# Indirect transfers and turned rows in place of selection matmuls for six of eight experts

## The reference

```python
def moe_swiglu(h, router, w_in, w_out):        # h = rms_norm(x, ffn_norm[1])
    t = h.reshape(b * s, d)
    logits = (t @ router).astype(jnp.float32)
    top_vals, top_idx = lax.top_k(logits, TOP_K)
    gates = jax.nn.softmax(top_vals, axis=-1)
    combine = jnp.sum(jax.nn.one_hot(top_idx, N_EXPERTS) * gates[..., None], axis=1)
    for e in range(N_EXPERTS):
        y = y + combine[:, e:e + 1] * swiglu(t, w_in[e], w_out[e])
```

## Time and profile before

| | us |
|---|---|
| median of 3 runs | 1492.41 (1492.3 to 1493.67) |
| the profiled execution, its own time | 1492.52 |
| its span in the trace | 1490.4 |
| PE busy | 1463.7 (98%) |
| DVE busy | 1208.6 (81%) |
| ACT busy | 995.7 (67%) |
| POOL busy | 132.8 (9%) |

### The profile page before, as it was taken

How to read it: one execution, slowest core, us unless ns; L and a number is a source line. 1 busy time by engine, 2 the same in 40 slices (tenths; PEclk the granted TensorE clock), 3 DMA queues, 4 the chain that set the end, 5 groups by cost and what they waited for, 6 DMA issues and landing times.

```text
span 1490.4 us, 19624 instructions
## 1 busy us (share of the span) xinstructions
PE 1463.7 (98%) x7818; PEld 1237.3 (83%) x7818; DVE 1208.6 (81%) x1031; ACT 995.7 (67%) x850; POOL 132.8 (9%) x201
## 2 busy tenths in 40 slices
PE   8999999999999999999999999999999999999998
PEld 7967888889998778888888888888888888888776
DVE  7976766666386799888888888888888888888997
ACT  5667444465546677777777777777777777777774
POOL 8505200000253000000000000000000000000200
PEclk9999999999999999999999999999999999999999
DMA  9504555546510399999999999999999999999994
GB/s 344 171 6 164 197 197 181 185 143 197 193 34 31 116 349 372 352 387 379 348 377 382 351 374 388 365 362 386 374 349 389 377 349 380 381 347 377 411 377 164
DMA packets 206919, 432.50 MB, mean 290 GB/s; under 512 B 6914, under 2 KB 56251, under 8 KB 206827
## 3 DMA queue, kind: packets, MB, share of 16 engines
q1 hardware_dynamic: 204880, 424.78, 78.2%
q0 software_dynamic: 1904, 6.46, 1.1%
q10 hardware_dynamic: 42, 0.01, 0.0%
HBM read 426.51 MB, written 4.72 MB: 289 GB/s over the span
## 4 chain that ended last, share of the span: by engine, by line
PE 92%; DVE 4%; ACT 2%; issue 1%; DMA 0%; DVEq 0%; SPq 0%; ACTq 0%
PE bank L1466 25%; PE bank L1468 25%; PE bank L1467 25%; PE bank L1507 6%; PE bank L1509 3%; PE bank L1739 2%; PE bank L1868 2%; PE bank L1820 1%; DVE w_l L294 1%; PE bank L1720 1%; DMA raw<-in_ab_w_in 0%; PE bank L1721 0%; ACT w_h L289 0%; PE bank L1567 0%; PE bank L1473 0%
## 5 line engine op out<-in xcount | busy, mean ns | idle before, releaser
L294 DVE TENSOR_TENSOR w_l<-raw,w_h 128x2048 fp32r<-128x2048 f32 x402 | 920.8, 2292 | 182.1 <-ACT w_h L289 181.4
L289 ACT ACTIVATE w_h<-raw 128x2048 fp32r<-128x2048 f32 x402 | 770.9, 1918 | 353.3 <-PE bank L1468 287.4
L1466 PE MATMUL bank<-w_h,hs_h 128*128 128x512 f32 x896 | 355.3, 397 | 3.7 <-DVE w_l L294 2.8
L1468 PE MATMUL bank<-w_h,hs_l 128*128 128x512 f32 x896 | 349.7, 390 | 0.0
L1467 PE MATMUL bank<-w_l,hs_h 128*128 128x512 f32 x896 | 349.0, 390 | 0.0
L1466 PEld LDWEIGHTS bank<-w_h,hs_h 128*128 128x128 f32 x896 | 168.3, 188 | 38.1 <-issue 3.3
L1468 PEld LDWEIGHTS bank<-w_h,hs_l 128*128 128x128 f32 x896 | 168.2, 188 | 36.0
L1467 PEld LDWEIGHTS bank<-w_l,hs_h 128*128 128x128 f32 x896 | 168.5, 188 | 33.2
L1466 PE MATMUL bank<-w_h,ma_h 128*128 128x512 f32 x448 | 174.6, 390 | 1.7 <-DVE w_l L294 1.7
L1467 PE MATMUL bank<-w_l,ma_h 128*128 128x512 f32 x448 | 174.3, 389 | 0.0
L1468 PE MATMUL bank<-w_h,ma_l 128*128 128x512 f32 x448 | 174.3, 389 | 0.0
(11 more groups left out here) (298 smaller groups left out, 1661.1 us busy)
## 6 DMA issues: line engine op xcount, KB each, us to landing
raw<-in_moe_w_in SPq DMA_DIRECT2D x224, 1024.0 KB, 5.7
raw<-in_moe_w_out SPq DMA_DIRECT2D x112, 1024.0 KB, 5.4
raw<-in_ffn_w_in SPq DMA_DIRECT2D x22, 1024.0 KB, 5.0
raw<-in_hgrn_w_in SPq DMA_DIRECT2D x16, 1024.0 KB, 5.1
raw<-in_ffn_w_out SPq DMA_DIRECT2D x11, 1024.0 KB, 4.7
raw<-in_ab_w_in SPq DMA_DIRECT2D x10, 1024.0 KB, 11.3
raw<-in_ab_w_out SPq DMA_DIRECT2D x4, 1024.0 KB, 4.8
raw<-in_hgrn_w_out SPq DMA_DIRECT2D x4, 1024.0 KB, 4.9
```

Source lines behind the costliest of these rows:

```text
L289: act.activation(w_h[:, u0 % S, :], raw[:, u0 % R, :], ACT.Copy).then_inc(w_high, 1)
L294: eng.tensor_tensor(w_l[:, u0 % S, :], raw[:, u0 % R, :], w_h[:, u0 % S, :], ALU.subtract).then_inc(w_low, 1)
L1466: pe.matmul(o, a_high, b_high, start=start, stop=False, skip_group_check=True)
L1468: return pe.matmul(o, a_low, b_high, start=False, stop=stop, skip_group_check=True)
```

## The change

- Early on POOL, three direct transfers copy `x` over most of a new tensor `x_rows` in device memory (768 rows).
- After the norm, ACT writes the scaled, ungained tokens to `xn` (`token_norm`). DVE works out for each token the slots of its two experts (`slots`, 14 small operations in step 0 of the first expert; a token without a slot gets a spare row). POOL sends `xn` to `x_rows` by four indirect transfers, waits for them, and loads 128 rows for each of the experts 1 to 6 into `x_g`, the first two at once, the others behind the writes of `y_rows`.
- For experts 1 to 6 PE turns those rows (`turn_rows`, eight transposes) in place of the 48 matmuls. Experts 0 and 7 are gathered as before; the first gather goes to four banks.
- The gain is put on behind the turning or the gather: `gather_high` and `gather_low` are eight operations of 128 columns with a scale each, where they were two of 512. The three bf16 parts are of ungained tokens; the third is made by POOL.
- The router reads `x` itself, turned, with the gain multiplied into its weights ahead of time and the norm applied to its 16 sums. The fillers `keep_warm` of the norm are gone and the eight after the router are four.
- `gates`, `slots`, `overflow`, `combine` and `rows` stand in steps 0 to 3 of the first expert, and ACT's Exp in step 1.

Cut to its core, with the lines that say the same for other buffers left out:

```diff
             n_const["all"] = made[0]
+            for b in range(3):
+                pool.dma_start(x_rows[CAP + b * T:CAP + (b + 1) * T, :], A["x"][0]).then_inc(x_fill, 16)
...
+            for tt in range(TT):
+                pool.wait_ge(x_mid, tt + 1)
+                pool.tensor_tensor(x_b[:, 2, tt, :], x_g[:, tt, :], x_b[:, 1, tt, :], ALU.subtract).then_inc(x_low, 1)
+            pool.wait_ge(x_norm, TT)
+            pool.wait_ge(x_fill, 16 * 3)
+            for k in range(2):
+                pool.wait_ge(slot_ok, k + 1)
+                for tt in range(TT):
+                    pool.indirect_dma_start(out=x_rows, out_offset=bass.IndirectOffsetOnAxis(ap=slot_i[:, k, tt:tt + 1], axis=0),
+                                            in_=xn[:, tt, :], in_offset=None).then_inc(x_sent, 16)
+            pool.wait_ge(x_sent, 16 * 2 * TT)
+            def expert_rows(e):
+                pool.dma_start(x_g[:, e % 2, :], x_rows[e * CAP:(e + 1) * CAP, :]).then_inc(xe_in[e % 2], 16)
+            expert_rows(1)
+            expert_rows(2)
             for e in range(NR):
                 pool.wait_ge(y_cp, 2 * e + 2)
                 pool.dma_start(y_rows[e * P:(e + 1) * P, :], y_f[:]).then_inc(y_out, 16)
+                if e + 3 < NE - 1:
+                    pool.wait_ge(m_gat, 2 * (e + 1) + 4)
+                    expert_rows(e + 3)
+            pool.wait_ge(m_gat, 2 * (NR - 1) + 4)
...
+            def residual_router():
+                add_part(3, 0, 0)
+                add_part(3, 0, 1)
+                norm_eps(3, 0)
+                add_part(3, 1, 0)
+                norm_root(3, 0)
+                add_part(3, 1, 1)
+                turned(0)
+                turned(1)
+                norm_eps(3, 1)
+                turned(3)
+                norm_root(3, 1)
+                token_rest(0)
+                token_rest(1)
...
+                    step(dve.tensor_tensor(row_m[:, 1 + k, :, :], logit[:, 4 + k, :, :], row_m[:, 0, :, :], ALU.mult))
+                    step(dve.tensor_tensor(row_m[:, 3, :, :], row_m[:, 1 + k, :, :], row_f[:], ALU.mult))
+                    dve.tensor_reduce(row_v[:, k, :], row_m[:, 1 + k, :, :], AX.X, ALU.max).then_inc(r_d, 1)
+                    done[0] += 1
+                    step(dve.tensor_reduce(row_w[:, k, :], row_m[:, 3, :, :], AX.X, ALU.add))
+                    step(dve.scalar_tensor_tensor(out=row_v[:, 2 + k, :], in0=row_v[:, k, :], scalar=0.5, in1=spill_no[:, k, :],
+                                                  op0=ALU.is_lt, op1=ALU.mult))
+                    dve.tensor_tensor(slot_i[:, k, :], row_v[:, 2 + k, :], row_w[:, k, :], ALU.add).then_inc(slot_ok, 1)
...
+            def gather_low(n, b, banks=(5, 6)):
+                w = KC // len(banks)
+                for k in range(KC):
+                    if k % w == 0:
+                        dve.wait_ge(m_hh, n * KC + (k + w))
+                    dve.scalar_tensor_tensor(out=hs_l[:, b, k, :], in0=bank[:, banks[k // w], (k % w) * P:(k % w + 1) * P],
+                                             scalar=par[:, C_FFN + 8 + k:C_FFN + 9 + k], in1=hs_h[:, b, k, :],
+                                             op0=ALU.mult, op1=ALU.subtract).then_inc(m_hl, 1)
...
+                if j == 0 and turn[0] == 0 and first:
+                    gates()
+                    slots()
+                if j in (1, 2, 3) and turn[0] == 0 and first:
+                    (overflow, combine, rows)[j - 1]()
+                if j == 3 and turn[0] and not last:
+                    dve.wait_ge(m_pt, q)
+                    choose(e + 1, 1, 1 - hb)
+                if j == 3 and turn[0] == 0 and e == NE - 2:
+                    choose(NE - 1, 0, 1 - hb)
...
-            for tt in range(TT):
-                act.wait_ge(x_gain, TT + tt + 1)
-                act.activation(x_b[:, 1, tt, :], x_g[:, tt, :], ACT.Copy).then_inc(x_mid, 1)
+            table(ACT.Sqrt)
+            norm_square(3, 0, 0)
+            norm_square(3, 0, 1)
+            norm_rms(3, 0)
+            norm_square(3, 1, 0)
+            token_high(0)
+            norm_square(3, 1, 1)
+            norm_rms(3, 1)
+            act.wait_ge(x_t, 3)
+            act.activation(h_f[:, 1, 0:4, :], bank[:, 2, :].rearrange("p (c t) -> p c t", c=4), ACT.Copy).then_inc(r_act, 1)
+            token_high(1)
+            token_mid(0)
+            token_mid(1)
             split_high(act, U_MOE + 2)
...
                 moe_gate(s + 1, u0 + 1, rounds)
+                if j == 1 and turn[0] == 0 and first:
+                    act.wait_ge(r_d, n_const["exp"])
+                    act.activation(pick[:, 5, :], pick[:, 4, :], ACT.Exp).then_inc(r_e, 1)
+                    table(ACT.Silu)
...
-            norm_turn(3)
...
+            for tt in range(TT):
+                pe.wait_ge(x_add, 8 + 2 * tt + 2)
+                for b in range(2):
+                    for c in range(4):
+                        last = pe.transpose(bank[:, 2 * tt + b, c * P:(c + 1) * P], x[:, tt, (4 * b + c) * P:(4 * b + c + 1) * P], ident[:])
+                    last.then_inc(x_t, 1)
+            pe.wait_ge(r_gain, 1)
+            for tt in range(TT):
+                for c in range(KC):
+                    if c % 4 == 0:
+                        pe.wait_ge(*((r_act, 1) if (tt, c) == (1, 0) else (r_dve, 2 * tt + c // 4 + 1 - tt)))
+                    last = pe.matmul(bank[:, 5, tt * NE:(tt + 1) * NE], h_f[:, tt, c, :], router[:, c, :],
                                      start=c + tt == 0, stop=c == KC - 1, skip_group_check=True)
             last.then_inc(r_lg, 1)
-            keep_warm(8, 7)
...
+            def turn_rows(e):
+                pe.wait_ge(xe_in[e % 2], 16 * ((e + 1) // 2))
+                for i in range(2):
+                    for c in range(4):
+                        last = pe.transpose(bank[:, 5 + i, c * P:(c + 1) * P], x_g[:, e % 2, (4 * i + c) * P:(4 * i + c + 1) * P], ident[:])
+                    last.then_inc(m_gat, 1)
...
                     k = half * KH + c
+                    if fresh is not None:
+                        pe.wait_ge(m_hl, fresh * KC + (k + 1))
                     last = three(bank[:, b, :], hs_h[:, hb, k, :], hs_l[:, hb, k, :], wh[:, c, :], wl[:, c, :], k == 0, k == KC - 1)
...
-                                pe.wait_ge(m_hl, n * 2 + 2)
-                            gather(n + 1, 1 - hb)
+                                pe.wait_ge(m_hl, n * KC + KC)
+                            if turn[0] == 0 and e + 1 < NE - 1:
+                                turn_rows(e + 1)
+                            else:
+                                gather(n + 1, 1 - hb, q + 3 if turn[0] else 2)
```

More of the change, by code:

```diff
@@ L42 @@
 NR = NE - 1
+SLOTS = NE * CAP
 LAM_INIT = 0.8 - 0.6 * math.exp(-0.3 * 0)
@@ L211, in build @@
         y_in = [sem(f"y_in{tt}") for tt in range(TT)]
+        x_norm, slot_ok, x_sent, x_fill = (sem(k) for k in "x_norm slot_ok x_sent x_fill".split())
+        xe_in = [sem(f"xe_in{b}") for b in range(2)]
         stored = sem("stored")
@@ L354, in _ @@
                            allow_small_or_imprecise_dtypes=True))
+            step(pool.iota(spill_no[:], pattern=[[T, 2], [P, TT]], base=SLOTS, channel_multiplier=1,
+                           allow_small_or_imprecise_dtypes=True))
             n_const["early"] = made[0]
@@ L935, in choose, with slots @@
                                       ALU.is_equal).then_inc(m_sel, 1)
-            def rows():
+            def slots():
                 ranks = rank[:].rearrange("p (a e) -> p a e", a=TT)[:, :, 0:NE]
                 step(dve.tensor_scalar(row_m[:, 0, :, :], ranks, CAP + 0.5, None, ALU.is_lt))
-                dve.tensor_tensor(row_f[:], ranks, row_no[:].unsqueeze(1).to_broadcast([P, TT, NE]), ALU.add).then_inc(r_d, 1)
-                done[0] += 1
+                step(dve.tensor_tensor(row_f[:], ranks, row_no[:].unsqueeze(1).to_broadcast([P, TT, NE]), ALU.add))
@@ new lines, in slots, with rows @@
+                    done[0] += 1
[3 more added lines that the diff above has]
+                    dve.tensor_tensor(slot_i[:, k, :], row_v[:, 2 + k, :], row_w[:, k, :], ALU.add).then_inc(slot_ok, 1)
+            def rows():
+                for k in range(2):
@@ L1007, in moe_body @@
                     row_sums(j // 2)
[L1008 to L1012, removed]
-                    choose(e + 1, turn[0], 1 - hb)
+                if j == 0 and turn[0] == 0 and first:
[8 more added lines that the diff above has]
+                    choose(NE - 1, 0, 1 - hb)
                 split_low(dve, u0 + 5, rounds)
@@ L1045, in moe_round @@
                         split_low(dve, u + i)
[L1046 to L1054 removed]
+                    gather_low(n0, 0)
+                for i in (3, 4, 5):
                     split_low(dve, u + i)
@@ L1826, in rows @@
                 def rows(i, parts, first, final):
-                    for c in range(4):
-                        f = slice((4 * i + c) * P, (4 * i + c + 1) * P)
```

(4 more changed lines are left out.)

191 lines of the change are left out of this document (87 added, 104 removed).

## The result

The changed kernel takes 1507.57 us (median of 4 runs, 1506.87 to 1507.87) against 1492.79 for the kernel before in the same comparison: a ratio of 1.0093, 95% interval 1.0081 to 1.0106. The prediction was 1479.1, range 1475 to 1486, with 0.07 on slower. It was wrong in sign.

The account below looks back on a forecast made before the run. PE was taken as the bound, busy 958.06 of 962.5 us at full clock in the expert stretch. The terms summed as 1492.5 - 11.2 - 3.4 + 0.7 + 0.5 = 1479.1 us, range 1475 to 1486.

Parts of the forecast that it names:

- a cut in PE's own list is worth its full length there: Expert stretch, 962.5 us with PE busy 958.06: instructions removed from PE save their whole time if ACT, DVE and DMA keep up.
- Turns, -11.2: Experts 1 to 6: eight fp32 turns of 0.93 us replace a 2.80 us gather, saving 1.87 each, 11.2 us in all.
- The beat of 17.7: Sign of being right: steps that held a gather take 17.7 us between SP's issues instead of 19.6.
- Small copies, 0: Eight 128-wide copies each on ACT and DVE behind the turns stay covered: 0, or up to 1 us at seven experts.
- Head, -3.4: From the last residual add to the first gather: shorter DVE chain, less a slower clock; 3.4 us saved, bounds -4.8 to -0.5.
- the head gives nothing: Rival, chance 0.15: half clock through gather and first weights, or x_low late, cancels the head's saving: 1482.5 us, or 1485.
- Small work in the first expert, +0.7: Gates' small operations moved into the first expert's steps: stalls of 4.3 us less 3.6 lost today, 0.7 us added.
- waits for w_l near 2, 1.7 and 0.4: Sign of being right: PE's waits in us in expert 0, from small operations put ahead of weights.
- clock below 1 behind 512 us: Sign of being wrong: PE's clock not full after 512 us, about when the first expert's matmul was expected.
- Traffic, +0.5: Added scatters, row loads and early copies crowd the weight loads: 0.5 us added, bounds 0 to 4.
- Rows late: Rival, chance 0.05: scatters taking over 60 us hold PE at expert 1; beyond 13 us late the kernel is slower.
- DMA is the bound: Rival, chance 0.05: at 365 GB/s the turns save nothing and 5.2 MB more cost 14.3 us: 1503.4 us.

Follow-up runs that it names:

- experiment 1: The changed kernel with the unused spare tensor 32 bytes smaller per partition, so the stage tensors start again at multiples of 512 bytes: 1483.71 us.
- experiment 10: experiment 1 with x_low made by VectorE behind the first expert's selection instead of by GpSimd: 1479.51 us.
- experiment 9: Program of only 512-column matmuls, none of the reference's work, tiles at varied starts: 389 ns at 0 or 256 bytes apart, 392 at 192, 394 to 396 else.

## Why the prediction was wrong

The step that failed is the first: "a cut in PE's own list is worth its full length there", with the 16.80 us of an ordinary step and the 2.72 of a unit carried over from the trace of before. The list did get shorter, by what was forecast. But the sum took every matmul that stays at its old length, and looked for costs only in waits and in instructions added. The diff's `spill_no` line was costed as "POOL's one more iota and DVE's scaling of the router are done while those engines wait", that is by its time and not by its place. Its place lengthened some 4400 matmuls by 6 ns each, 24 us in all (experiment 1).

The account, in medians: 1479.1 predicted + 23.9 (experiment 1) + 4.2 (experiment 10) = 1507.2, measured 1507.57. It closes because experiment 10 lands on the forecast, and that is in part luck. Its profiled execution (1479.39 us) against the one before (1492.52) goes by four pieces: up to the first expert's matmul 515.47 - 512.46 = 3.0 us less (forecast 3.4); from there to the second expert's turns, which stand at

```profile
595.51 1.03 PE L1898 MATMUL bank<-ident,x_g 128*128 128x128 f32 x8
```

83.05 us where the gather came after 81.71, 1.3 more (forecast 0.7); from there to the end 882.2 for 893.2, 11.0 less (forecast 11.2 less 0.5 for traffic, 10.7); and 1.7 us outside the trace for 2.1. No piece is off by more than 0.7, but they cancel to 0.3. Point by point:

- *Turns, -11.2*: right. Eight turns cost 0.89 to 0.93 us over two steps, and the gather 2.80. The beat of 17.7 that was named as the sign was off in shape (17.95, then 16.58) and right in sum. One turn's record is 0.27 us long, but eight begin within 0.8 us: what counts is the distance of their starts.
- *Small copies, 0*: right. No wait for `hs_l` in experts 1 to 6.
- *Head, -3.4*: wrong as run, by one term. "x_low, which goes from DVE to POOL", was called hidden because PE comes to it late enough; what it does to DVE meanwhile was not asked. POOL's two operations took 2.2 each, as costed, but held up DVE's selection by 3.5 us (1.82 + 2.21 for 0.57), and by 3.1 in experiment 1. There the first expert starts at 515.51, as before the change (515.47): the outcome of the rival "the head gives nothing" (1482.5, measured 1483.71), by a cause that it didn't name. With that undone, the sums are read at 503.94 (forecast 504.8), the gather starts at 507.14 (508.0), and the first expert's matmul stands at 512.46 (512.1). Inside it, the clock was under-costed: the gather took 4.87 where 3.03 + 0.8 was taken. An earlier start paid for it.
- *Small work in the first expert, +0.7*: mis-sized: half of what came. The signs were waits for w_l near 2, 1.7 and 0.4. Experiment 10 has two in the first expert, 3.6 us of its 5.3, the longest 2.1, and the stretch above grew by 1.3. The changed kernel has 3.1 of its 4.3 there (its longer beat hides more). The fall of its clock behind the wait of 1.81 is one of the signs of being wrong that the prediction named ("clock below 1 behind 512 us"); it is worth 1.4 us, and the runs don't show why experiment 1 was spared.
- *Traffic, +0.5*: no cost seen. PE waits for nothing but DVE, and 374 GB/s in the expert stretch of experiment 1 stand against 365:

```profile
515.50:1468.00 952.50, 947.23 (x4335) 782.04 (x4336) 851.62 (x555) 718.66 (x526) 22.54 (x21) 1.00 1.00 374
```

- *Rows late*: no wait of PE for `x_g` in any trace.
- *The rival "DMA is the bound"*, 1503.4, lies nearest to the result and is the wrong reason. Anyone who had stopped at the number, at a DMA share of 0.99 and at an unchanged 365 GB/s in the changed kernel, would have taken it. But experiment 1 moved 374 GB/s with the same transfers, and the old kernel slowed down equally with none.

What stays open: why the 512-column matmuls of the dense layer (L1507, `w_h` stationary, `h_hl` moving), whose tiles begin a multiple of 512 bytes apart, take 398 ns in the kernel before, 394 with the weights moved, and 392 with only the stage tiles moved by 64 bytes, which neither of the two is. So the distance of the two tiles does not settle every case. Against the 399 with 32 bytes that is 352 x 7 ns = 2.5 us, the difference between those two runs; but with 128 bytes it is 396, and the time is no longer than with 64. Why 192 bytes cost only half was not tried. Nor was it tried whether POOL's work could stay on POOL if it began behind the selection.

## What to carry to other kernels

In a kernel at 98% PE, a new tensor can change every matmul whose tiles are allocated behind it: compare the mean ns of the unchanged matmuls before looking for waits, and add small tensors at the end of the allocation or in slots that keep the old starts. Moving work to an idle engine is free only if the operations that it runs beside are not on the path; name the other engine's instructions in that stretch and their operands. When a result agrees in size with one of the rivals, still undo that rival's cause alone.

## What the runs showed of the hardware

- fp32r matmuls of 512 columns, 128x128 stationary: 389 ns in the trace if the stationary and the moving tile start 0 or 256 bytes apart in SBUF (experiment 9, past a multiple of 512), 394 to 396 at most other distances tried (32, 64, 96, 128, 160, 224, -32), 392 at 192. Back to back that is 16.80 against 17.22 us for a step of 72. It needs no other engine. In bf16 there is no difference (379 at 0, 32 and 128).
- A GpSimd subtraction of 128x1024 with two SBUF inputs and a VectorE comparison of 128x128 with two SBUF inputs, begun during it: the latter takes 1.5 to 2.2 us for 0.29. A VectorE operation with one of its inputs in PSUM kept its 0.17.
- The granted clock was 0.50 (1.2 of 2.4 GHz) from 506 to 510 us in experiment 10, after the 32 router matmuls of 8 columns and 0.69 us idle, and with two more fillers of 512 columns in that gap 0.50 from 506 to 508 and 0.97 from 508 on.
- Behind a wait of 1.81 us in the first expert the granted clock of the changed kernel fell to 0.50 for some 3 us; behind the longest waits of experiments 1 and 10, 2.0 and 2.1 us in the same stretch, it stayed at 1.00.
